# Three edits in one kernel: values of attention by token, logits and row minima in one instruction, last normalisation by a column of tokens

## The reference

```python
logits = jnp.einsum('bhqd,bhkd->bhqk', q_i, k).astype(jnp.float32) * ATTN_SCALE
logits = logits + f_i[..., :, None] - fcum[..., None, :]        # or + a bias by distance
logits = jnp.where(kpos[None, :] <= qpos[:, None], logits, -jnp.inf)
p = jax.nn.softmax(logits, axis=-1)
return jnp.einsum('bhqk,bhkd->bhqd', p.astype(v.dtype), v)
```

```python
def rmsnorm_2(x, g):
    xf = x.astype(jnp.float32)
    y = xf * lax.rsqrt(jnp.mean(xf * xf, axis=-1, keepdims=True) + EPS)
    return (y * g.astype(jnp.float32)).astype(x.dtype)
```

## Time and profile before

| | us |
|---|---|
| three runs | 960.65, 957.74, 961.14 |
| median | 960.65 |
| profiled execution, whole | 957.83 |
| its span, first to last instruction | 955.6 |
| TensorE busy | 930.6 |
| VectorE busy | 663.7 |
| ScalarE busy | 525.6 |
| GpSimd busy | 184.3 |
| attention stages, about | 283 to 390 and 597 to 706 |

### The profile page before, as it was taken

How to read it: one execution, slowest core, us unless ns; L and a number is a source line. 1 busy time by engine, 2 the same in 40 slices (tenths; PEclk the granted TensorE clock), 3 DMA queues, 4 the chain that set the end, 5 groups by cost and what they waited for, 6 DMA issues and landing times.

```text
span 955.6 us, 20828 instructions
## 1 busy us (share of the span) xinstructions
PE 930.6 (97%) x7618; PEld 908.9 (95%) x7618; DVE 663.7 (69%) x1177; ACT 525.6 (55%) x847; POOL 184.3 (19%) x90
## 2 busy tenths in 40 slices
PE   8899999999998999999999999999999999999995
PEld 8889999999997999999999999989989999999994
DVE  6998666667556776676666765798558777785566
ACT  6346755554444555575555544556557766664353
POOL 3430444430000001034444000000202444410001
PEclk9999999999999999999999999999999999999997
DMA  7435855557532533365556653344335555566421
GB/s 260 174 137 201 251 198 187 183 207 265 173 132 89 177 134 132 124 235 191 176 178 203 229 182 132 123 155 143 110 111 177 198 178 188 187 215 212 168 83 45
DMA packets 46328, 163.51 MB, mean 171 GB/s; under 512 B 5010, under 2 KB 9746, under 8 KB 46277
## 3 DMA queue, kind: packets, MB, share of 16 engines
q1 hardware_dynamic: 41704, 158.19, 48.5%
q10 hardware_dynamic: 4573, 4.62, 1.8%
HBM read 161.71 MB, written 3.44 MB: 173 GB/s over the span
## 4 chain that ended last, share of the span: by engine, by line
PE 88%; DVE 8%; ACT 2%; issue 1%; DMA 1%; SPq 0%; DVEq 0%; ACTq 0%
PE psum L1255 28%; PE psum L1256 27%; PE psum L1257 27%; DVE work L894 2%; DVE wl L797 1%; PE psum L1427 1%; DMA raw<-in_even_in 1%; PE psum L1404 1%; PE psum L1396 1%; ACT wh L492 1%; PE psum L1368 0%; PE psum L1366 0%; ACT work L653 0%; DVE work L836 0%; DVE acc L865 0%
## 5 line engine op out<-in xcount | busy, mean ns | idle before, releaser
L1255 PE MATMUL psum<-xs,wh 128*128 128x256 f32 x1632 | 466.7, 286 | 2.5 <-DVE wl L797 2.5
L1256 PE MATMUL psum<-xs,wh 128*128 128x256 f32 x1632 | 462.4, 283 | 0.0
L1257 PE MATMUL psum<-xs,wl 128*128 128x256 f32 x1632 | 462.3, 283 | 0.0
L492 ACT ACTIVATE wh<-raw 128x1024 fp32r<-128x1024 f32 (+2 forms) x270 | 301.2, 1120 | 270.2 <-PE psum L1257 260.3
L797 DVE TENSOR_TENSOR wl<-raw,wh 128x1024 fp32r<-128x1024 f32 (+2 forms) x197 | 262.8, 1336 | 108.8 <-ACT wh L492 108.4
L1255 PEld LDWEIGHTS psum<-xs,wh 128*128 128x128 f32 x1632 | 313.6, 192 | 8.5 <-issue 4.2
L1256 PEld LDWEIGHTS psum<-xs,wh 128*128 128x128 f32 x1632 | 313.7, 192 | 0.2
L1257 PEld LDWEIGHTS psum<-xs,wl 128*128 128x128 f32 x1632 | 313.7, 192 | 0.0
L442 POOL TENSOR_TENSOR wl<-raw,wh 128x1024 fp32r<-128x1024 f32 x73 | 176.5, 2418 | 656.9 <-ACT wh L492 656.8
L1255 PE MATMUL psum<-ys,wh 128*128 128x256 f32 x672 | 191.8, 285 | 0.0
L1256 PE MATMUL psum<-ys,wh 128*128 128x256 f32 x672 | 190.8, 284 | 0.0
(11 more groups left out here) (194 smaller groups left out, 689.9 us busy)
## 6 DMA issues: line engine op xcount, KB each, us to landing
raw<-in_up SPq DMA_DIRECT2D x132, 512.0 KB, 3.3
raw<-in_down SPq DMA_DIRECT2D x48, 704.0 KB, 4.1
raw<-in_qkv SPq DMA_DIRECT2D x48, 512.0 KB, 3.2
raw<-in_even_in SPq DMA_DIRECT2D x16, 512.0 KB, 4.2
raw<-in_out SPq DMA_DIRECT2D x16, 512.0 KB, 3.2
raw<-in_ple SPq DMA_DIRECT2D x8, 640.0 KB, 3.8
raw<-in_even_out SPq DMA_DIRECT2D x8, 512.0 KB, 3.2
toeplitz_dram<-table_dram ACTq DMA_DIRECT2D x1, 2048.0 KB
```

The costliest lines, as they stand in the source:

```text
L492: nc.scalar.activation(split_weights(q, s, tiles * P)[0], raw[:, s, 0:tiles * P], ACT.Copy).then_inc(hi_ready, 1)
L1255: nc.tensor.matmul(bank, high_w[:, w], high, start=first, stop=False)
L1256: nc.tensor.matmul(bank, high_w[:, w], low, start=False, stop=False)
L1257: done = nc.tensor.matmul(bank, low_w[:, w], high, start=False, stop=last)
```

## The change

**Values by token.** The weights of two pairs' values are laid out together on the host (`projection_units`): 256 output channels, and the eight input tiles in two halves. Units 6g + 2 and 6g + 3 carry them; six units are two pairs: q, k, values, values, q, k. `value_unit` takes 128 tokens of `xs` as the stationary operand and 256 columns of weights as the moving one, so the values come out tokens by channels, in one whole PSUM bank for both pairs. They need no transposing. Their norm's factor then belongs to the partition: `turn_rstd` turns `rstd` to a column by two small matmuls, VectorE copies it (`read_token_rstd`), and ScalarE reads the values with it as a scale (`read_values`, two instructions for two pairs). Banks are counted by `bank_use`. Since k of an odd pair is now the last unit before that pair's scores, `scores_behind` puts one unit ahead of the scores of odd pairs. The first two units of a stage wait until every bank of the phase before is read.

**Logits.** The table of biases is multiplied by 8 beforehand. One `tensor_tensor_reduce` per head and block of tokens adds bias and score, multiplies by -1/8 and takes the row minimum, and ScalarE's exponential has scale -1.

**The last normalisation.** ones and squares change places in the last statistics, so that each token's sum is one element of a column, 128 x 2. Root and reciprocal are on two columns; two matmuls with a broadcast column and the identity spread it over the partitions, into PSUM. VectorE squares the last chunk and does all eight multiplications; GpSimd has none. The square root's table is loaded ahead of the statistics. The stores are four of two chunks.

```diff
-        EARLY = QKV_BANKS
+        token_bank = psum[:, 6, SPAN:SPAN + 2]
+
+
+
+        def is_value(u):
+            return u % 6 in (2, 3)
+
+        def bank_use(u):
+            return 5 * (u // 6) + (0, 1, 2, 2, 3, 4)[u % 6]
+
+        def reads_to(use):
+            return 4 * (use // 5) + (1, 2, 2, 3, 4)[use % 5]
 
         def qkv_bank(u):
-            return turned_banks[:, 0, 0:SEQ] if u == EARLY else psum[:, u % QKV_BANKS, 0:SEQ]
+            return psum[:, bank_use(u) % QKV_BANKS, 0:2 * SEQ if is_value(u) else SEQ]
+
+        def scores_behind(kind, n):
+
+            return n % 2 == 1 or kind == "stick"
...
-                    source = stick_values if order[n][0] == "stick" else turned_banks[:, :, SPAN:SPAN + P]
-                    nc.scalar.activation(qkv[:, 3 * n + 2, :].rearrange("p (b d) -> p b d", b=2), source, ACT.Copy)\
-                      .then_inc(turned_read, 1)
+                def read_values(g):
+
+                    u = 6 * g + 3
+                    act.wait_ge(units_done, base[name] * RING + u + 1)
+                    act.wait_ge(token_ready, layer + 1)
+                    for b in range(2):
+                        last = nc.scalar.activation(qkv[:, u - 1:u + 3:3, b * P:(b + 1) * P],
+                                                    qkv_bank(u)[:, b * SEQ:(b + 1) * SEQ].rearrange("p (c d) -> p c d", c=2),
+                                                    ACT.Identity, scale=token_rstd[:, b:b + 1])
+                    last.then_inc(values_read, 1)
...
                     round_ahead("ple", i, s)
                     act.wait_ge(ple_in, m + 1)
                     nc.scalar.activation(ple_s[:, m % 2, 0:SEQ], ple_z[:, m % 2, 0:SEQ], ACT.Sigmoid).then_inc(ple_gate, 1)
-                    act.wait_ge(h_final, m + 1)
-                    wait_square(7, m)
-                    square_chunk(7, m, m % 2)
                     if m == DC - 1:
-                        norm_root(7)
+
+                        nc.scalar.preload_act_table(ACT.Sqrt)
+                        act.wait_ge(square_ready, DC * 8)
+                    else:
+                        act.wait_ge(h_final, m + 1)
+                        wait_square(7, m)
+                        square_chunk(7, m, m % 2)
...
-                    first = steps.mark(nc.vector.scalar_tensor_tensor(e[:, :, 0:P], S[:, :, 0:P], HD ** -0.5, b[:, :, P:SEQ],
-                                                                      ALU.mult, ALU.add))
-                    second = steps.mark(nc.vector.scalar_tensor_tensor(e[:, :, P:SPAN], S[:, :, P:SPAN], HD ** -0.5, b,
-                                                                       ALU.mult, ALU.add))
-                    steps.wait(first)
-                    nc.vector.tensor_reduce(row_max[:, n % 2, 0:2], e[:, :, 0:P], AX.X, ALU.max, negate=True)
-                    steps.wait(second)
-                    last = nc.vector.tensor_reduce(row_max[:, n % 2, 2:4], e[:, :, P:SPAN], AX.X, ALU.max, negate=True)
+
+                    for half in range(2):
+                        b = bias[:, HEADS if kind == "fox" else 2 * (c - 4) + half, :]
+                        for block, (a, z, first) in enumerate(((0, P, P), (P, SPAN, 0))):
+                            at = 2 * block + half
+                            last = nc.vector.tensor_tensor_reduce(e[:, half, a:z], S[:, half, a:z], b[:, first:SEQ], -HD ** -0.5,
+                                                                  -NEG, ALU.add, ALU.min, row_max[:, n % 2, at:at + 1])
...
-            dve.wait_ge(root_ready, 8)
-            nc.vector.reciprocal(rstd[:, :], root).then_inc(last_scale, 1)
-            dve.wait_ge(last_scale, 1)
-            for m in range(POOL_OUT, DC):
+            dve.wait_ge(h_final, DC)
+            dve.wait_ge(square_used, DC * 8 - 1)
+            nc.vector.tensor_tensor(squares(7, 1)[:, 0, :], h[:, DC - 1, :], h[:, DC - 1, :], ALU.mult).then_inc(square_ready, 1)
+            dve.wait_ge(last_rooted, 1)
+            nc.vector.reciprocal(last_rstd[:, :], last_root[:, :]).then_inc(last_scale, 1)
+            dve.wait_ge(last_spread, 1)
+            for m in range(DC):
                 dve.wait_ge(gained, m + 1)
-                nc.vector.tensor_tensor(h[:, m, :], h[:, m, :], rstd[:, :], ALU.mult).then_inc(out_ready, 1)
+                nc.vector.tensor_tensor(h[:, m, :], h[:, m, :], last_rows, ALU.mult).then_inc(out_ready, 1)
...
+                def value_unit(u):
+
+                    s, bank, first = u % RING, qkv_bank(u), u % 6 == 2
+                    pe.wait_ge(lo_ready[s], q0 + u // RING + 1)
+                    for i in range(DC // 2):
+                        t, w = i + (0 if first else DC // 2), slice(i * SEQ, (i + 1) * SEQ)
+                        for b in range(2):
+                            tokens, sums = slice(b * P, (b + 1) * P), bank[:, b * SEQ:(b + 1) * SEQ]
+                            nc.tensor.matmul(sums, xs[:, t, 0, tokens], wh[:, s, w], start=first and i == 0 and b == 0, stop=False,
+                                             skip_group_check=True)
+                            nc.tensor.matmul(sums, xs[:, t, 0, tokens], wl[:, s, w], start=False, stop=False, skip_group_check=True)
+                            last = nc.tensor.matmul(sums, xs[:, t, 1, tokens], wh[:, s, w], start=False,
+                                                    stop=not first and i == DC // 2 - 1, skip_group_check=True)
+                    last.then_inc(units_done, 1)
+
+                def turn_rstd():
+
+                    pe.wait_ge(rstd_ready, n_norm + 1)
+                    for b in range(2):
+                        last = nc.tensor.matmul(token_bank[:, b:b + 1], rstd[:, b * P:(b + 1) * P], ident[:, 0:1], start=b == 0, stop=True,
+                                                skip_group_check=True)
+                    last.then_inc(token_turned, 1)
...
                 def turn(n):
 
                     N = PAIRS * layer + n
-                    pe.wait_ge(bank_read, q0 * RING + max(3 * n + 3, EARLY + 1))
-                    if n >= 1:
-                        pe.wait_ge(turned_read, N)
-                    for b in range(2):
-                        target = stick_values[:, b, :] if order[n][0] == "stick" else turned_banks[:, b, SPAN:SPAN + P]
-                        nc.tensor.transpose(target, qkv[:, 3 * n + 2, b * P:(b + 1) * P], ident[:, :])
...
-                begin(q0, (0, 1), qkv_bank, lambda s: q0 * RING + s - QKV_BANKS + 1, from_xs,
+                begin(q0, (0, 1), qkv_bank, lambda s: q0 * RING, from_xs,
                       lambda t: pe.wait_ge(xl_ready, DC * n_norm + t + 1))
...
                 for j in range(1, PAIRS):
-                    late = order[j - 1][0] == "stick"
+                    behind = scores_behind(order[j - 1][0], j - 1)
                     if j == 1:
-                        qkv_unit(EARLY)
-                    if not late:
+                        qkv_unit(3)
+                    if not behind:
                         scores(j - 1)
-                    if j > 1:
+                    if j == 1:
+                        turn_rstd()
+                    else:
                         qkv_unit(3 * j)
-                    if late:
+                    if behind:
                         scores(j - 1)
...
             pe.wait_ge(square_used, DC * 8 - 1)
-            pe.wait_ge(bank_read, total * RING)
-            nc.tensor.matmul(stat, ones[:, :], acc[:, :], start=True, stop=False)
+            for b in range(2):
+                nc.tensor.matmul(last_stat[:, b:b + 1], acc[:, b * P:(b + 1) * P], ones[:, 0:1], start=b == 0, stop=False,
+                                 skip_group_check=True)
             pe.wait_ge(square_ready, DC * 8)
-            nc.tensor.matmul(stat, ones[:, :], squares(7, (DC - 1) % 2)[:, 0, :], start=False, stop=True).then_inc(stat_ready, 1)
+            for b in range(2):
+                last = nc.tensor.matmul(last_stat[:, b:b + 1], squares(7, 1)[:, 0, b * P:(b + 1) * P], ones[:, 0:1], start=False, stop=True,
+                                        skip_group_check=True)
+            last.then_inc(stat_ready, 1)
+            pe.wait_ge(last_scale, 1)
+            for b in range(2):
+                last = nc.tensor.matmul(last_rows[:, b * P:(b + 1) * P], last_rstd[:, b:b + 1].to_broadcast([P, P]), ident[:, :],
+                                        start=True, stop=True)
+            last.then_inc(last_spread, 1)
```

106 lines of the change are left out of this document (72 added, 34 removed).

## The result

| | before, us | after, us |
|---|---|---|
| median (lowest to highest), 5 runs each | 960.12 (957.74 to 961.14) | 951.36 (949.75 to 953.58) |
| ratio, 95% interval | | 0.9913 [0.9892, 0.9935] |
| the same two kernels, compared again later | 958.65 | 952.11, ratio 0.9939 [0.9923, 0.9956] |
| profiled execution: whole, span | 957.83, 955.6 | 951.67, 949.5 |

The change gained more than was forecast: 0.6 to 0.9%, where it was 0.5%. The two profiled executions differ by 6.1 us of span, and that is what the traces can account for.

The account below looks back on a forecast made before the run. TensorE, busy 97% of the span, was taken as the bound. Terms -2.6 transposes, -1.2 first turns, -0.6 copied values, +1.7 new wait, -2.3 end sum to -5.0; from 960.65 that forecast 955.6 us, range 951.8 to 961.5.

Parts of the forecast that it names:

- The end: After the last addition into h: column statistics, short root and reciprocal, eight multiplications on VectorE alone; 2.3 us less.
- The new wait at the stages' starts: First unit of each attention stage waits for all reads of the stage before: 0.83 us lost each, 1.7 us together.
- The transposes: TensorE's two value transposes per pair go: 0.22 us at each of twelve turns, 2.6 us gained.
- rival (b): Value units run at a longer pace with token blocks stationary, making the kernel slower; 971 us at 0.16 us per matmul; chance 0.08.
- The wait on the copied values: TensorE's 0.6 us wait for ScalarE's copy L671, which is removed: 0.6 us gained.
- The logits and the first turns: Logits 1.53 us instead of 1.86, and one read-out fewer: each stage's first turn 0.6 us sooner, 1.2 us together.
- The second pair of stage 2: Its turn was given no gain from the transposes, because VectorE's key read-out is late there.
- The odd pairs' place: Odd pairs' scores move behind a unit, leaving two units before the turn: fits by 0.1 to 0.2 us, costs nothing.
- The signs that it named: If right: 0.9 us gap before each stage's first projection matmul, 1.8 us first-turn wait in stage 1, end 9 us.
- (c): More gained: last turn and odd pairs keep 0.22 us, end gives 3 us, relieved VectorE shortens waits; 952.8 us; chance 0.13.
- (a): The combined logits pass is slow, logits 2.6 us: 961.7 us, halfway 958.5; chance 0.12.
- (d): The attention part does nothing, each 0.22 us coming back as a wait for VectorE: 958.9 us; chance 0.15.

Follow-up runs that it names:

- the alone-run: Only the last normalisation by a column of tokens, put on the kernel before: ratio 0.9981 [0.9966, 0.9995], 956.6 us; the end took 9.06 us instead of 11.24.

## Why the prediction fell short

Most signs and places were right, and several sizes to a tenth. The step that failed is the price of the logits: 0.33 us less was forecast for their chain, and it is 0.74. Two terms that stood at nothing were wrong as well: the second pair of stage 2 (0.75 us gained), which hangs on the logits, and, apart from them, the new place of the odd pairs' scores (0.2 us at each of three). The sum was 1.8 us too small (5.0 for 6.8): about 0.5 at the first turns, 0.75 at that second pair and 0.7 by the odd pairs' place, less 0.2 that came back as a wait. It was also counted from runs that stood 2.6 us high. Point by point:

- **The end: right.** -2.2 us for a forecast of -2.3. The pace of 0.67 us was misread (one row averaged over two paces, 0.34 and 0.86), but the sum did not use it. The multiplications' pace of 0.33 us and the column form's times (1.02, 0.26, 0.17, 1.22) came as worked out from the rows of before; the alone-run says the same.
- **The new wait at the stages' starts: right.** +0.8 and +0.9 us for +0.83 each; taking it out gives both back.
- **The transposes: right.** The even pairs of stage 1 come 0.20 to 0.22 us sooner each, and the last turn of stage 2 waits 0.2 us for VectorE as forecast. The value units kept their pace; rival (b), the one on the slow side, had nothing in it.
- **The wait on the copied values: right.** The weighing that waited 0.6 us in the earlier trace rows comes 0.65 us sooner.
- **The logits and the first turns: the step that failed, by its size.** The forecast compared 1.86 us with 1.53. The traces say 1.97 and 1.23: 0.74 us, not 0.33. The missing 0.4 us is the read of the accumulator, taken at 0.12 us each (between a bound of 0.06 and ScalarE's 0.186): it lasts 0.083 us but runs under the pass behind it and adds 0.01 to 0.02 to the pace, so the four cost 0.4 us less. Both chains end 0.11 us later than their paces add up to (1.97 for 1.86, 1.23 for 1.12), which cancels. The count of instructions, which the prediction held against this part, did not decide: eight took less than four. With 0.33 for the read-out that went, 0.74 gives 1.07, and the first turn came 1.06 us sooner. In stage 2 the first turn gained 0.66 us, about all that it had waited (0.7 in the earlier trace rows): from there TensorE itself is the bound, and the 0.6 forecast fits.
- **The second pair of stage 2: failed as a consequence.** It was given nothing, because VectorE was late there. The turn gained 0.75 us: 0.22 are its transposes, and the rest goes with the wait for ScalarE's squares (`diff`) ahead of it, which the forecast didn't name. It is 0.21 us in the kernel before and 0.54 with the values alone, and it is gone in the kernel after and with the logits alone, which take 0.47 us out of this stretch. So it is the shorter logits that let both engines keep up. The following scores got 0.2 us of it back as a wait (0.9 instead of 0.7 us, L1366 in the earlier trace rows for the line of before). The logits alone take 1.5 us out of stage 2.
- **The odd pairs' place: "cost nothing" was wrong.** It does fit, as worked out, and no scores wait for a key in stage 1. But it was priced only for what it might delay. The earlier trace rows hold one of the seams: six transposes 0.11 us apart from 342.73 on, then the scores at 343.48, 0.09 us behind the pace. There are two seams fewer, 0.2 us at each of three pairs. The kernel before with this edit alone confirms the size in stage 1, and that stage 2 gains nothing by it.
- **The signs that it named.** The gap ahead of the first projection matmul was 0.78 us (0.9 forecast), the first turn's wait 1.43 (1.8), the end 9.01 (9).
- **What is left.** Stage 1 gained 3.44 us: 1.06 + 7 x 0.22 + 3 x 0.2, and 0.1 at the last odd pair, make 3.3. I have no row for the other 0.1.
- **The base.** -5.0 was set against a median of three runs, and that they stood high is bad luck. The median of 31 is 958.05; with the change's 6.8 us that gives 951.3, where 951.36 was measured. More than half of the distance between 955.6 and 951.36 is this base (2.6 us), the rest the sizes above (1.8).

Of the rivals, (c), "more is gained", with 952.8 us was the nearest. Of its three reasons one held, that a relieved VectorE shortens further waits, and one in part: the odd pairs kept their 0.22 us, while the last turn of stage 2 waits 0.2 us. The end did not give 3 us. (a) fell with 0.42 us per combined pass of 256, (d) with the 0.22 us that stayed at the even pairs.

## What to carry to other kernels

Price a move of work on the bottleneck engine for its neighbours as well as for its dependences: count the seams between kinds of work before and after, and read a seam's price where the timeline's step departs from the steady pace. A chain is measured from its first start to the start of what waits for it, in both kernels; a small step inside it may lie wholly under its neighbour, so the lower bound deserves as much weight as the upper. And where the bottleneck engine waits long in one place, look there first: shortening that wait is worth its length and at times as much again, because the clock behind it may be lower.

## What the runs showed of the hardware

- VectorE's combined add, scale and row minimum takes 0.287 us over 128 and 0.420 over 256 elements, as long as scale and addition alone (0.41 for 256 in the earlier trace rows); its accumulator is read in 0.083 us, under the following instruction.
- VectorE's multiplication of two SBUF tiles of 128x256 takes 0.42 us alone and 0.94 to 0.95 us while GpSimd does the same work (kernel before, the end).
- Between matmuls over 128 rows into 128 columns (float32 projection, transposes) and matmuls over 64 rows or into 64 columns TensorE loses about 0.1 us in each direction: steps of 0.20 to 0.22 us for 0.11 or 0.12. Between projection and transposes it loses nothing (0.12 us).
- Some waits of TensorE were followed by the lower granted clock, 0.50, for 3 to 4 us, and some were not. At the first turn of stage 1: 2.16 us of waiting, clock 0.50 over the 3.3 us behind it; 3.00 us, 0.55; at a cost of 1.5 us each. But 1.00 behind 2.38 us (three profiles), 1.94 us (one) and 1.43 us (four). In the first 100 us of all twelve profiles a wait of 2.6 us, at 37.5 to 40.2 us, is followed by the lower clock, for twice as long in three of them. Near 67 us a wait of 2.2 us is followed by it in ten, and one of 1.75 us, in the other two, is not. What decides stays open.
